# Feed forward with wide products: x kept with its high and low parts side by side, five matmuls a chunk

## The reference

```python
def swiglu(h, wg, wu, wd):
    return (jax.nn.silu(h @ wg) * (h @ wu)) @ wd
...
        yp = yp + swiglu(rmsnorm(yp, norm_ffn[layer]), w_gate[layer], w_up[layer], w_down[layer])
        ys = ys + swiglu(rmsnorm(ys, norm_ffn[layer]), w_gate[layer], w_up[layer], w_down[layer])
```

## Time and profile before

| what | value |
|---|---|
| median of 3 runs | 1392.13 us (1391.37 to 1396.53) |
| the profiled execution, its time | 1395.11 us |
| its span, first to last instruction | 1392.9 us |
| TensorE busy with matmuls | 1336.7 us (96%) |
| VectorE busy | 654.2 us (47%) |
| ScalarE busy | 435.6 us (31%) |
| GpSimd busy | 174.2 us (13%) |
| mean granted clock of TensorE | 0.982 |
| DMA | 115.07 MB, mean 83 GB/s |

### The profile page before, as it was taken

How to read it: one execution, slowest core, us unless ns; L and a number is a source line. 1 busy time by engine, 2 the same in 40 slices (tenths; PEclk the granted TensorE clock), 3 DMA queues, 4 the chain that set the end, 5 groups by cost and what they waited for, 6 DMA issues and landing times. The chain is left out here.

```text
span 1392.9 us, 25321 instructions
## 1 busy us (share of the span) xinstructions
PE 1336.7 (96%) x10450; PEld 1279.4 (92%) x10450; DVE 654.2 (47%) x925; ACT 435.6 (31%) x669; POOL 174.2 (13%) x170
## 2 busy tenths in 40 slices
PE   7878888999999999999999999999999999999998
PEld 6767666999999999999989888899999999999998
DVE  5738674744443244445553334277544432344422
ACT  6332463232222122232324334452322221222211
POOL 4993000510000000003200000005100000000000
PEclk9989899999999999999999999899999999999999
DMA  6456020343333223332221211123333232232332
GB/s 173 103 76 120 18 65 1 95 137 90 90 98 93 76 80 91 90 98 84 62 62 47 59 52 49 47 77 107 91 90 90 86 101 85 76 90 78 106 95 73
DMA packets 231689, 115.07 MB, mean 83 GB/s; under 512 B 34564, under 2 KB 228568, under 8 KB 231592
## 3 DMA queue, kind: packets, MB, share of 16 engines
q1 hardware_dynamic: 229208, 113.46, 29.5%
q10 hardware_dynamic: 2416, 0.70, 0.5%
HBM read 107.77 MB, written 7.38 MB: 83 GB/s over the span
## 5 line engine op out<-in xcount | busy, mean ns | idle before, releaser
L315 PE MATMUL ps<-xh,whi 128*128 128x272 f32 x1408 | 291.7, 288 | 2.1 <-DVE wlo L274 2.1
L315 PE MATMUL ps<-xh,wlo 128*128 128x272 f32 x1408 | 291.4, 288 | 0.0
L315 PE MATMUL ps<-xl,whi 128*128 128x272 f32 x1408 | 290.2, 288 | 0.0
L315 PEld LDWEIGHTS ps<-xh,whi 128*128 128x128 f32 x1408 | 221.6, 188 | 2.6 <-issue 2.5
L315 PEld LDWEIGHTS ps<-xl,whi 128*128 128x128 f32 x1408 | 221.3, 188 | 0.0
L315 PEld LDWEIGHTS ps<-xh,wlo 128*128 128x128 f32 x1408 | 219.8, 189 | 0.0
L274 DVE TENSOR_TENSOR wlo<-wraw,whi 128x1024 fp32r<-128x1024 f32 (+1 forms) x118 | 165.2, 1400 | 98.4 <-ACT whi L269 93.9
L269 ACT CAST whi<-wraw 128x1024 fp32r<-128x1024 f32 (+1 forms) x118 | 133.2, 1129 | 139.8 <-PE ps L315 139.8
L315 PE MATMUL ps<-hh,whi 128*128 128x272 f32 x704 | 145.7, 288 | 0.0
L315 PE MATMUL ps<-hl,whi 128*128 128x272 f32 x704 | 145.4, 288 | 0.0
L315 PE MATMUL ps<-hh,wlo 128*128 128x272 f32 x704 | 145.4, 288 | 0.0
(11 more groups left out here) (539 smaller groups left out, 1960.4 us busy)
## 6 DMA issues: line engine op xcount, KB each, us to landing
wraw<-in_w_gate SPq DMA_DIRECT2D x88, 256.0 KB, 3.0
wraw<-in_w_up SPq DMA_DIRECT2D x88, 256.0 KB, 3.1
wraw<-in_w_down SPq DMA_DIRECT2D x32, 384.0 KB, 3.8
wraw<-in_w_in_odd SPq DMA_DIRECT2D x48, 256.0 KB, 3.1
wraw<-in_w_down SPq DMA_DIRECT2D x32, 320.0 KB, 3.2
wraw<-in_w_in_even SPq DMA_DIRECT2D x20, 256.0 KB, 4.8
wraw<-in_w_out_odd SPq DMA_DIRECT2D x16, 256.0 KB, 3.0
ev_xs<-in_x_prompt SPq DMA_DIRECT2D x4, 512.0 KB, 6.0
```

The lines of the kernel that those rows point to most:

```text
L315: ins = pe.matmul(K.ps[:, 2 * s + h, 0:HT], w[s][:, k, :], a[:, k, h * HT:(h + 1) * HT], start=start, stop=stop)
```

## The change

The kernel is the same but for the feed forward and the splitting of x ahead of it.

- **x** lies in one tensor `xx` in the place of `xh` and `xl`, 1088 columns a chunk: high part of the first half (272) and 92 columns of low part, the same again for the second half, then the other 360 columns of the low part. The hidden chunks lie the same way in `hx`, but for the second half of layer 1, which stays as it was (`wide`).
- **A chunk** is five matmuls: `whi` with 364, 364 and 360 columns, and `wlo` with 272 and 272. The 184 and 360 columns of `whi·xl` no longer accumulate on top of `whi·xh`: the former go to columns 272 to 363 of the slot's two banks, the latter to a third bank, 4 or 5.
- **Taking a panel out**: ScalarE copies the low columns out of PSUM in two copies into `low`, VectorE adds the slot's two banks to them, and what was one read of PSUM by VectorE (times `rstd`, or added to `resid`) becomes a second operation.
- **Splitting** x and the hidden chunk takes one activation as before and three operations on VectorE in place of one.
- In layer 1 the first panel waits for the third update of `ml_c`, since it uses banks 4 and 5.

```diff
+LOW = 92
+WIDE = HT + LOW
...
+def multiply_wide(K, pe, g, a, before_chunk=None, midway=None):
+    def body(i):
+        for s in g.slots:
+            pe.wait_ge(K.lo_ready[s], g.n[s] + i + 1)
+            pe.wait_ge(K.acc_free[s], g.n[s] + i)
+            for k in range(g.kc):
...
+                first, last = k == 0, k == g.kc - 1
+                for h in range(2):
+                    pe.matmul(K.ps[:, 2 * s + h, 0:WIDE], K.whi[s][:, k, :], a[:, k, h * WIDE:(h + 1) * WIDE], start=first, stop=False)
+                pe.matmul(K.ps[:, 4 + s, 0:2 * T - 2 * WIDE], K.whi[s][:, k, :], a[:, k, 2 * WIDE:2 * T], start=first, stop=last)
+                for h in range(2):
+                    ins = pe.matmul(K.ps[:, 2 * s + h, 0:HT], K.wlo[s][:, k, :], a[:, k, h * WIDE:h * WIDE + HT], start=False, stop=last)
+            ins.then_inc(K.panel_done[s], 1)
...
+def split_wide_lo(K, dve, norm, m):
...
+    dve.scalar_tensor_tensor(pair, two(x), gain, two(high[:, 0, :]), ALU.mult, ALU.subtract)
+    dve.scalar_tensor_tensor(rest[:, 0:HT - 2 * LOW], x[:, 2 * LOW:HT], gain, high[:, 0, 2 * LOW:HT], ALU.mult, ALU.subtract)
+    dve.scalar_tensor_tensor(rest[:, HT - 2 * LOW:], x[:, HT:T], gain, high[:, 1, :], ALU.mult, ALU.subtract)\
+        .then_inc(K.sem("x_lo"), 1)
...
+    wide = [True, layer == 0]
...
             if half == 0:
-                multiply_panels(K, pe, g_up[0], K.xh, K.xl, wait_x(K, pe, norm), rms)
+                if layer:
+                    pe.wait_ge(sem("ml_c_new"), 3)
+                multiply_wide(K, pe, g_up[0], K.xx, wait_x(K, pe, norm), rms)
...
             def evac(s, i):
                 take(K, dve, g_up[half], s, i)
+                turn = low_turns[half] - FH + i + 1
+                dve.wait_ge(low_taken[s], turn * 2)
+                dve.tensor_tensor(halves(low[s][:]), K.acc[s], halves(low[s][:]), ALU.add).then_inc(K.acc_free[s], 1)
+                dve.wait_ge(K.acc_free[s], g_up[half].n[s] + i + 1)
                 if s == sg:
...
-                    dve.tensor_tensor(halves(gate[:]), K.acc[s], halves(K.rstd[:]), ALU.mult).then_inc(K.acc_free[s], 1)
+                    dve.tensor_tensor(gate[:], low[s][:], K.rstd[:], ALU.mult).then_inc(gate_ready, 1)
                 else:
...
-                    dve.tensor_tensor(halves(up[:]), K.acc[s], halves(K.rstd[:]), ALU.mult).then_inc(K.acc_free[s], 1)
-                    dve.wait_ge(K.acc_free[s], g_up[half].n[s] + i + 1)
+                    dve.tensor_tensor(up[:], low[s][:], K.rstd[:], ALU.mult).then_inc(scaled, 1)
+                    dve.wait_ge(scaled, n + i + 1)
                     dve.wait_ge(gated, n + i + 1)
                     dve.tensor_tensor(up[:], up[:], act_gate[:], ALU.mult).then_inc(hid, 1)
...
+        def take_low(s):
+            act.copy(low[s][:, 0:2 * LOW].rearrange("p (a t) -> p a t", a=2), K.ps[:, 2 * s:2 * s + 2, HT:WIDE]).then_inc(low_taken[s], 1)
+            act.copy(low[s][:, 2 * LOW:T], K.ps[:, 4 + s, 0:T - 2 * LOW]).then_inc(low_taken[s], 1)
...
             def evac(s, i):
+                take(K, act, g_up[half], s, i)
+                take_low(s)
```

More of the change, by code:

```diff
@@ L1858, in phase_ffn @@
     hh, hl = r(f"hh{layer}", [P, FH, T], F32R), r(f"hl{layer}", [P, FH, T], F32R)
+    hx = Region(nc, K.scratch_at)(f"hx{layer}", [P, FH, 2 * T], F32R)
     gate, up, act_gate = (r(f"{x}{layer}", [P, T]) for x in ("gate", "up", "act_gate"))
+    low = [r(f"low{x}{layer}", [P, T]) for x in range(2)]
+    low_taken = [sem(f"low_taken{x}") for x in range(2)]
+    low_added = [sem(f"low_added{x}") for x in range(2)]
+    wide = [True, layer == 0]
     norm = 2 * layer + 1
@@ L1870, in phase_ffn @@
     turns = [FH * (2 * layer + half) for half in range(2)]
+    low_turns = [(2 * layer + half) * (FH + DC // 2) + FH for half in range(2)]
+    gate_ready, scaled = sem("gate_ready"), sem("up_scaled")
     def two_loads(half):
@@ L1959, in _ @@
             else:
-                multiply_panels(K, pe, g_down[half], hh, hl, before)
+                multiply_wide(K, pe, g_down[half], hx, before)
     @block.vector
@@ L1964, in add_resid @@
         def add_resid(g, last):
+            half = int(last)
             def evac(s, i):
@@ L1968, in evac @@
                 x = chunk(K.resid, m)
-                dve.tensor_tensor(halves(x), K.acc[s], halves(x), ALU.add).then_inc(K.acc_free[s], 1)
+                if wide[half]:
+                    dve.wait_ge(low_taken[s], (low_turns[half] + i + 1) * 2)
+                    dve.tensor_tensor(low[s][:], low[s][:], x, ALU.add).then_inc(low_added[s], 1)
+                    dve.wait_ge(low_added[s], (DC // 2) * (2 * layer + half) + i + 1)
+                    dve.tensor_tensor(halves(x), K.acc[s], halves(low[s][:]), ALU.add).then_inc(K.acc_free[s], 1)
+                else:
+                    dve.tensor_tensor(halves(x), K.acc[s], halves(x), ALU.add).then_inc(K.acc_free[s], 1)
                 if last and layer == 0:
@@ L1997, in evac @@
                     dve.wait_ge(hid_hi, n + i + 1)
-                    dve.tensor_tensor(chunk(hl, i), up[:], chunk(hh, i).bitcast(F32), ALU.subtract).then_inc(hid_lo, 1)
+                    if wide[half]:
+                        t = chunk(hx, i)
+                        pair, rest = low_parts(t)
+                        high = high_part(t).bitcast(F32)
+                        dve.tensor_tensor(pair, up[:, 0:2 * LOW].rearrange("p (a t) -> p a t", a=2),
+                                          high[:, 0, 0:2 * LOW].rearrange("p (a t) -> p a t", a=2), ALU.subtract)
+                        dve.tensor_tensor(rest[:, 0:HT - 2 * LOW], up[:, 2 * LOW:HT], high[:, 0, 2 * LOW:HT], ALU.subtract)
+                        dve.tensor_tensor(rest[:, HT - 2 * LOW:], up[:, HT:T], high[:, 1, :], ALU.subtract).then_inc(hid_lo, 1)
+                    else:
+                        dve.tensor_tensor(chunk(hl, i), up[:], chunk(hh, i).bitcast(F32), ALU.subtract).then_inc(hid_lo, 1)
             split_and_take(K, dve, g_up[half], split_lo, evac, g_down[half], True, int(half == 0))
@@ L2009, in evac @@
             def evac(s, i):
+                take(K, act, g_up[half], s, i)
+                take_low(s)
                 if s == sg:
-                    act.wait_ge(K.acc_free[s], g_up[half].n[s] + i + 1)
+                    act.wait_ge(gate_ready, n + i + 1)
                     if not (isinstance(i, int) and n + i == 0):
@@ L2016, in evac @@
                     act.wait_ge(hid, n + i + 1)
-                    act.copy(chunk(hh, i), up[:]).then_inc(hid_hi, 1)
+                    if wide[half]:
+                        act.copy(high_part(chunk(hx, i)), halves(up[:])).then_inc(hid_hi, 1)
+                    else:
+                        act.copy(chunk(hh, i), up[:]).then_inc(hid_hi, 1)
             def after_down(s, i):
                 m = i * 2 + slots.index(s)
+                if wide[half]:
+                    take(K, act, g_down[half], s, i)
+                    take_low(s)
+                if not half:
+                    return
                 if layer == 0:
@@ L2029, in _ @@
             split_and_take(K, act, g_up[half], split_hi, evac, g_down[half], True, int(half == 0))
-            split_and_take(K, act, g_down[half], split_hi, after_down if half else None,
+            split_and_take(K, act, g_down[half], split_hi, after_down,
                            g_up[1] if half == 0 else g_next, True, down_pairs(half))
@@ L2947, in _ @@
                 split_lo_of(dve, W_OUT + c + 2)
-            split_x_lo(K, dve, 3, [c])
+            split_wide_lo(K, dve, 3, c)
             if c == 0:
```

28 lines of the change are left out of this document (24 added, 4 removed).

## The result

| what | before | changed |
|---|---|---|
| median of 8 runs | 1396.04 us (1391.37 to 1399.43) | 1404.32 us (1399.94 to 1405.63) |
| ratio | 1 | 1.0058, 95% interval 1.0038 to 1.0077 |
| span of the profiled execution | 1392.9 us | 1403.0 us |
| VectorE, ScalarE busy | 654.2, 435.6 us | 743.4, 508.8 us |

The change makes the kernel slower by 8.3 us, 0.6%. The time forecast was 1407.9, the range 1385 to 1422. The median of before over these runs is 3.9 us above that of the first three, so of the +15.8 us that were forecast, 8.3 are there. The sign, the place and the kind of the loss were right, and its size was half. That 1407.9 stands only 3.6 us from 1404.3 is in part luck: the forecast started from a median that was 3.9 us low. Runs of one kernel differ with their mean granted clock, in the kernel before from 1391.1 us at 0.984 to 1400.1 at 0.976.

A forecast was written before the change was run, and what follows sets the result against it. TensorE's own time sets the pace, with the up chain only 0.95 us from making it wait. −11.6 + 25.3 + 2.1 = +15.8 us on the profiled 1395.1 gives 1410.9; the median, 3.0 lower, 1407.9 us, range 1385 to 1422.

The forecast's parts named there:

- the up chain's slack: Steps from an up panel's evacuation to the slot's next weights on TensorE: 4.68 us, 0.95 us to spare.
- Term A: Gate, up and down: 968 chunks made wide, each saving one matmul's fixed 12.0 ns, −11.6 us.
- rivals 2 and 3: Matmul price by columns, saving 0, 1415.9 us, chance 0.08; or weight loads sticking out, saving 48 ns, 1384.0 us, chance 0.12.
- Term B: Gate and up loop: TensorE waits 0.665 us for the up chain's weights in 38 pairs, +25.3 us.
- the added operation: Up chain: one more VectorE operation, adding and multiplying by `rstd` being now two, 0.76 us, high end 0.85.
- the three subtractions: Up chain: VectorE makes the hidden chunk's low part in three operations, adding 0.05 us, ends 0 and 0.25.
- Term C: Feed forward entries: first evacuation 0.9 us later in two layers, sum of squares 0.3 us later in layer 1, +2.1 us.
- The clock: TensorE at full clock has gaps of at most 0.7 us in 12.5, so nothing was added.
- Rival 1: Up slot: the chain lengthens by 0.85 us or less, nothing waits, −9.5 us, 1382.6 us, chance 0.10.
- The down products: Down panels: new work stays covered by over 3 us, 264 × 12 ns saved whole, panels 8.18 us without a gap.

The follow-up runs named there:

- pad1: The kernel before with one more VectorE operation of 544 columns in the up chain, its result unused: 1396.1 us, ratio 1.0004.
- pad2: The kernel before with two more VectorE operations of 544 columns in the up chain, their results unused: 1410.7 us, ratio 1.0111.
- narrow_early: The kernel before with next panel's weights split earlier, in each layer's first pair even ahead of the root mean square: 1400.6 us, ratio 1.0034.

## Why the prediction was right, and where its size was off

**What bounds.** Right. The bound was the up chain's slack, not any engine's load. The slack was taken as 0.95 us for the kernel before; pad1 and pad2 put it near 1.1.

**Term A, −11.6 us.** Right. TensorE of the changed kernel in time, in the second half of an up panel (503.81 to 509.8):

```profile
508.38 0.49 PE L1880 MATMUL ps<-xx,whi 128*128 128x364 f32 x2
508.71 0.33 PE L1881 MATMUL ps<-xx,whi 128*128 128x360 f32 x1
508.87 0.41 PE L1883 MATMUL ps<-xx,wlo 128*128 128x272 f32 x2
509.12 0.49 PE L1880 MATMUL ps<-xx,whi 128*128 128x364 f32 x2
```

A chunk takes 509.12 − 508.38 = 0.74 us, as forecast (0.752 − 0.012). VectorE in two down panels:

```profile
646.56 0.73 DVE L2042 TENSOR_TENSOR resid<-ps,low 128x544 f32<-128x544 f32 x1
...
654.70 0.72 DVE L2042 TENSOR_TENSOR resid<-ps,low 128x544 f32<-128x544 f32 x1
```

They stand 8.14 us apart, 11 chunks of 0.74, where 8.18 were forecast. In time, the wide products bring 12.4 us where nothing waits in the loop. The price of a matmul has a part that doesn't go with its columns; rivals 2 and 3 fall, since a chunk saved neither 0 nor 48 ns. The prediction also weighed the rule of the Trainium skill (TensorE: Matmul & The Clock Gate, Back-to-back issue gap) that a warm matmul costs its columns plus 2.5 ns. The page gives it for an isolated matmul. It doesn't describe this stream of weight loads and matmuls, where the excess is 12 ns.

**Term B, forecast 25.3 us, measured 16.9.** This is the step that was off in size. 38 pairs wait, as forecast, each 12.285 − 11.84 = 0.445 us instead of 0.665. The forecast spacing was 12.505, and its 0.22 too much came in three parts, each a hand-off or an overlap read from one row:

- *Start of the evacuation to the end of `wlo`*: 6.08 forecast, 5.99 measured. The copies and their hand-off took more (0.78 against 0.71). But the second product follows the first after 0.76, not the 0.85 of before, since the listing's register operation no longer stands between; the prediction used this for the added operation and forgot it for the old one. And the three subtractions cost nothing (1.63 from the high part to `wlo`, 1.64 before), where 0.05 was counted.
- *`wlo` to TensorE*: 0.06 us in the loop, where the row at the entry gave 0.12.
- *TensorE's start to the next evacuation*: 6.25 us, where 6.305 was forecast, since ScalarE starts on a finished panel some 0.06 us earlier than VectorE did.

None of the three is more than 0.09 us, and 38 pairs made 8.4 us of them.

**Term C, forecast 2.1 us, measured 2.2.** The gaps in front of the third panels grew from 1.31 to 2.24 us between starts, 0.93 each against 0.9, and the one at the root mean square of layer 1 by 0.3.

**The clock, forecast 0, estimated at 3.4 us in the profile** (two stretches of 3.4 us at half clock). The sentence that failed is that TensorE has gaps of 0.7 us at most. It was true of the loop, but term C itself had put 0.9 us on a gap of 1.3, and nobody asked what a gap of 2.2 us does to the clock.

Together −11.6 + 16.9 + 2.2 + 3.4 = 10.9 us, against 10.1 between the two spans. The agreement is no finer than 2 us or so, since the two executions were also at half clock for different times elsewhere. The medians, 8.3 us apart, can't be split up in this way.

**The rivals.** Rival 1 named an added 0.85 us as the point that decides the sign. By the prediction's own terms only the wait begins there; the sign turns 9.5/38 = 0.25 us later, at 1.10, when the wait has used up the gain. In the changed kernel, whose panels are 0.096 us shorter, the chain grew by 5.99 − 4.56 = 1.43 us and 0.445 of them became wait, so the wait begins at 0.985. The down products had no gap and gained, as forecast.

## What to carry to other kernels

When a change takes work from the busiest engine and gives it to two that are half idle, lay out the chain of in-order steps between a panel's end and the next weights, and compare it with the time of one panel: a busy share of 47% says nothing about it. Then look for steps of that chain that don't need the one ahead of them; here moving the weights' split in front of two waits turned a loss of 8 us into a gain of 15. And before putting a step early in an order, see when its data are asked for and land: an in-order engine that waits for a DMA holds back all behind it.

## What was not expected of the hardware

- At the entries of the feed forward, gaps of 1.2 to 1.7 us between TensorE's matmuls left the clock at 2.4 GHz in every trace here, and gaps of 2.2 us and more were followed by 3.4 us at 1.2 GHz. These began between 0.4 us before work resumed (narrow_early, 1002.4 against 1002.78) and 1.4 us after it (296.51 to 297.9). Elsewhere 2.75 us of idle time at the same place were followed by 1.2 GHz in pad1 and not in the kernel before. A gap's length alone doesn't tell.
- A matmul of 364 columns takes 0.165 us (508.71 − 508.38 = 0.33 for two), some 13 ns above its columns at 2.4 GHz; one of 272 takes 12 above. So the fixed price is nearly the same at both widths.
